# Moving the normed inputs of three groups of projections to 64 bytes above the weights' place within 512 bytes

## The reference, cut to what matters

```python
# first block, for each of 2 layers
xn = rms_norm(h, attn_norm_g[layer]);  proj = xn @ w_in[layer]          # 1024 -> 2304
...                                                                     # S5, gMLP, differential attention
h = h + mixed @ w_out[layer]
xn = rms_norm(h, ffn_norm_g[layer])
up = xn @ w_up[layer]                                                   # 1024 -> 5632
acc = causal_conv3(up);  gate, val = split(acc)
h = h + (gelu(gate) * val) @ w_down[layer]                              # 2816 -> 1024
# second block
h2 = rms_norm(x, g_pre)
a_qkv, bq, bk, bv, mq, ga, gb, gm, mg = split(h2 @ w_in_2)              # 1024 -> 10496
kvm = rms_norm(mem, g_mem) @ w_mem_kv                                   # 1024 -> 1024
ya, yb, ym = (o * silu(g)) @ w_br for the three branches
out = (sum of sigmoid(mg) * y) @ w_out_2;  x = x + rms_norm(out, g_post)
```

## The kernel before, in words

| input | read by | place | above the weights |
|---|---|---|---|
| `xth`, `xtl` | mixer's inputs, `out`, all first-level projections of the second block, `wo` | 128 | 0 |
| `fth`, `ftl` (same memory, 8 floats on) | up projections | 160 | 32 |
| `memh`, `meml` | `km`, `vm` | 128 | 0 |
| `hth`, `htl` | `down` | 128 | 0 |
| `oth`, `otl` | branches | 128 | 0 |

## Time and profile before

### The profile page before, as it was taken

One profiled execution on the slowest core, in us unless ns is written; L12 is line 12 of the kernel. 1 busy time (PEld: TensorE's weight loads), 2 busy tenths in 40 slices (PEclk: granted clock), 3 DMA queues, 4 the chain that ended last, 5 costly groups with the idle time before them and its releaser, 6 DMA issues.

```text
span 964.3 us, 15784 instructions
## 1 busy us (share of the span) xinstructions
PE 953.3 (99%) x6119; PEld 837.1 (87%) x6123; DVE 687.4 (71%) x1081; ACT 567.6 (59%) x960; POOL 232.1 (24%) x189
## 2 busy tenths in 40 slices
PE   8999999999999999999999999999999999999997
PEld 6887899999888888899999988999778889888886
DVE  7987878786765877857777754748576755666885
ACT  7967666676855657756666544535454445555733
POOL 5560203536500110302445500021131300000030
PEclk9999999999999999999999999999999999999999
DMA  8642466656664634466566565665545445754462
GB/s 299 227 131 68 142 219 186 189 178 184 194 197 152 180 127 153 133 188 192 180 194 178 195 196 154 216 202 173 166 139 153 153 144 170 199 162 155 154 180 82
DMA packets 48618, 165.96 MB, mean 172 GB/s; under 512 B 6560, under 2 KB 7072, under 8 KB 48544
## 3 DMA queue, kind: packets, MB, share of 16 engines
q1 hardware_dynamic: 48544, 164.95, 54.9%
HBM read 162.83 MB, written 1.05 MB: 170 GB/s over the span
## 4 chain that ended last, share of the span: by engine, by line
PE 88%; ACT 4%; POOL 3%; DVE 3%; issue 1%; DMA 1%; SPq 0%; DVEq 0%; POOLq 0%; ACTq 0%
PE PJ L655 14%; PE PJ L657 13%; PE PJ L656 13%; PE PJ L648 10%; PE PJ L647 10%; PE PJ L646 10%; PE PJ L593 2%; PE PJ L603 2%; PE PJ L586 2%; PE T L1118 1%; ACT sm L1378 1%; PE T L1109 1%; ACT whi L1177 1%; DMA raw<-weights_in 1%; DVE wlo L1873 1%
## 5 line engine op out<-in xcount | busy, mean ns | idle before, releaser
L1873 DVE TENSOR_TENSOR wlo<-raw,whi 128x1024 fp32r<-128x1024 f32 x294 | 368.7, 1284 | 87.2 <-ACT whi L1177 84.8
L1177 ACT ACTIVATE whi<-raw 128x1024 fp32r<-128x1024 f32 x294 | 301.6, 1059 | 64.9 <-DMA raw<-weights_in 62.5
L646 PE MATMUL PJ<-xthb,whi 128*128 128x256 f32 x832 | 233.7, 281 | 0.0
L648 PE MATMUL PJ<-xthb,wlo 128*128 128x256 f32 x832 | 233.4, 281 | 0.0
L647 PE MATMUL PJ<-xtlb,whi 128*128 128x256 f32 x832 | 232.4, 279 | 0.0
L655 PE MATMUL PJ<-whi,xthb 128*128 128x512 f32 (+1 forms) x424 | 170.8, 403 | 0.3 <-DVE wlo L1873 0.2
L657 PE MATMUL PJ<-whi,xtlb 128*128 128x512 f32 (+1 forms) x424 | 164.0, 387 | 0.0
L656 PE MATMUL PJ<-wlo,xthb 128*128 128x512 f32 (+1 forms) x424 | 164.0, 387 | 0.0
L647 PEld LDWEIGHTS PJ<-xtlb,whi 128*128 128x128 f32 x832 | 157.0, 189 | 0.3
L646 PEld LDWEIGHTS PJ<-xthb,whi 128*128 128x128 f32 x832 | 157.0, 189 | 0.3
L648 PEld LDWEIGHTS PJ<-xthb,wlo 128*128 128x128 f32 x832 | 156.9, 189 | 0.0
(11 more groups left out here) (419 smaller groups left out, 1353.2 us busy)
## 6 DMA issues: line engine op xcount, KB each, us to landing
raw<-weights_in SPq DMA_DIRECT2D x294, 512.0 KB, 3.6
rt<-bmerge_in SPq DMA_DIRECT2D x6, 256.0 KB, 4.1
memx<-mem_in SPq DMA_DIRECT2D x2, 512.0 KB, 4.0
y_out<-xn SPq DMA_DIRECT2D x4, 256.0 KB, 2.3
rowv<-rows_in SPq DMA_DIRECT2D x1, 576.0 KB, 10.5
xres<-x_in SPq DMA_DIRECT2D x2, 256.0 KB, 3.0
xres<-x_in SPq DMA_DIRECT2D x1, 512.0 KB, 7.7
ptmp<-bexp_in SPq DMA_DIRECT2D x2, 256.0 KB, 6.0
```

Source lines behind the costliest of these rows:

```text
L646: pe.matmul(o, a, xh[:, k, :], start=(first and f % 2 == 0), stop=False, skip_group_check=True)
L648: m = pe.matmul(o, b, xh[:, k, :], start=False, stop=last, skip_group_check=True)
L1177: act.activation(whi[:, p % HIGHS, :], raw[:, p % LOADS, :], ACT.Copy).then_inc(hi_ready, 1)
L1873: dve.tensor_tensor(wlo[:, p % LOADS, :], raw[:, p % LOADS, :], whi[:, p % HIGHS, :].bitcast(F32), ALU.subtract).then_inc(lo_ready, 1)
```

## The change

The instructions, their order on every engine and their waits stay as they were; only addresses change.

- `fth`, `ftl` lie 16 floats (64 bytes) into `xthb`, `xtlb`, where they lay 8.
- The second block's normed tokens (norm 5) are written to `fth`, `ftl` and read from there, where they were in `xth`, `xtl`.
- `lines` is 64 bytes longer: `memh`, `meml` go to 192, and with them every tile that is allocated behind `lines`: the first block's tables and mixer tiles, and the second block's `sm2`, `pT2`, `rt`, `gat`, `ma`, `gt` and others, all 64 bytes up.
- `lines1` and `lines2` are 64 bytes shorter, so that `hth`, `htl`, `acc`, `gtd` and `aqT`, `va`, `oth`, `otl`, `merged`, `gpost` keep their places.

Afterwards `fth`, `ftl`, `memh`, `meml` are at 192, 64 above the weights, whether they move (features first) or stand still (tokens first); `xth`, `xtl`, `hth`, `htl`, `oth`, `otl` stay at 0 above.

```diff
-                                  for o in (0, 8))
+                                  for o in (0, 16))
...
-        sbt(ctx, "lines", [P, 120])
+        sbt(ctx, "lines", [P, 136])
...
-        sbt(ffs, "lines1", [P, 96])
+        sbt(ffs, "lines1", [P, 80])
...
-        sbt(two, "lines2", [P, 96])
+        sbt(two, "lines2", [P, 80])
...
-            project("mq", fm=True, ready=(sem("xt_lo"), 80, 4))
-            project("bq")
-            project("gb", fm=True)
-            project("bkv")
+            project("mq", fm=True, xh=fth, xl=ftl, ready=(sem("xt_lo"), 80, 4))
+            project("bq", xh=fth, xl=ftl)
+            project("gb", fm=True, xh=fth, xl=ftl)
+            project("bkv", xh=fth, xl=ftl)
...
-            project("gm", fm=True)
+            project("gm", fm=True, xh=fth, xl=ftl)
...
-                    project(nm, pairs=[j], fm=nm == "ga")
+                    project(nm, pairs=[j], fm=nm == "ga", xh=fth, xl=ftl)
...
-                project(f"mg{n // 4}", pairs=[n % 4])
+                project(f"mg{n // 4}", pairs=[n % 4], xh=fth, xl=ftl)
...
-                xh = memh if n == MEM_NORM else fth if n in FFN_NORM else xth
+                xh = memh if n == MEM_NORM else fth if n in FFN_NORM or n == 5 else xth
...
-                xh, xl = (memh, meml) if n == MEM_NORM else (fth, ftl) if n in FFN_NORM else (xth, xtl)
+                xh, xl = (memh, meml) if n == MEM_NORM else (fth, ftl) if n in FFN_NORM or n == 5 else (xth, xtl)
```

## The result

The changed kernel took 969.54 us (median of 5 runs, 968.94 to 970.09), the kernel before 965.80 (5 runs, 965.09 to 966.09): ratio 1.0039, 95% interval 1.0028 to 1.0050. It is slower by 3.7 us. The forecast said 971.3 us and slower; the time lies in the range, but not for the reason given: that it came out near the forecast is luck.

A forecast was written before the change was run, and what follows sets the result against it. TensorE, busy 953.3 of 964.3 us, was taken as the bound, so start-to-start distances count one for one. Terms 5.8 - 0.4 = +5.4 us on 965.9 gave 971.3 us, range 956 to 973.

The forecast's parts named there:

- step 5: Everything else shifted 64 bytes behind `lines`, attention matmuls, transposes and other engines' tiles: 0, ends 1 us either way.
- step 4: Tokens-first matmuls leaving place 0 (768, `vm` 48, `bkv` 48 half width): stay at 226 ns, 0; end +3.4 us.
- step 1: Features-first up projections of both layers, 2016 matmuls: from 116.3 to 117.6 ns up to 120, +5.8 us.
- Step 2: First up chunk, tokens first, 48 matmuls: back from 234 to 226 ns, -0.4 us.
- Step 3: Features-first `km`, `mq`, `gb`, `gm`, `ga` leaving place 0, 480 matmuls: stay at 120 ns, 0.
- the prediction's own sign: In `a` and `mg` chunks, bursts behind attention: settling at 227 ns supports no tokens-first cost, staying at 233 refutes it.
- only place 0 is special: Every other place is like 32: up projections 117 ns, the 480 -1.3 us, tokens first +3.4; 968.0 us, chance 0.13.
- The first rival: Each further 32 bytes act like the first for the moving operand: 114.4 ns, 957.6 to 961.0 us; chance 0.37.
- The change does nothing: Tile identity or surrounding instruction order counts, not place, in all the moved products: 965.9 us, chance 0.05.
- the agreement on which I built: Tokens first, stationary operand: cost above 213 ns rises 13 to 20 ns as two 64-byte pieces become three.
- the -3 ns of the moving operand: Features first: moving input 32 bytes above the weights takes about 3 ns off each start-to-start distance.

The follow-up runs named there:

- a_sec64: Kernel before, with only the second block's normed tokens moved from 0 to 64 bytes above the weights: 967.74 us, ratio 1.0024.
- b_all_up64: Kernel before, with an unused 64-byte tile ahead of all others, so places shift but distances between operands stay: 965.72 us, ratio 1.0002.
- c_scan1: Kernel before, inputs at other distances: layer 0 up projections 16 bytes, layer 1 128, memory 128, second block 512: 965.99 against 965.69 us.
- d_scan2: Kernel before, inputs at other distances: layer 0 up projections 480 bytes, layer 1 16, memory 256, second block 496: 967.35 against 964.98 us.
- e_up448: Kernel before, with both layers' up-projection input at 448 (64 bytes below the weights) instead of 32 above: 958.6 us, ratio 0.9924.
- f_best: `e_up448` with the second block's tokens at 448 too, memory at 0: 960.23 us, ratio 0.9940 against the kernel before.
- e_all448: Kernel before, with layer 0's input and the memory at 192, layer 1's and the second block's at 448: 962.34 us, ratio 0.9963.

## Why the prediction was right or wrong

The sign was right, the mechanism was not. The forecast rested on the sentence that the operand's start counts within pieces of 64 bytes, so that 64 would be the same as 0. Every term fell but step 5, and the sum came near only because step 4 cost, at its end, much of what step 1 did not. That is luck.

- **Step 1**, +5.8 us, failed: the up projections went to 117.8 ns and not to 120, +1.0 us. (The 116.3 ns of its 288 matmuls is a count's error; by the starts they ran at 116.7.) Layer 0 left the rhythm of 116.7 for that of 117.8, which layer 1 had all along.
- **Step 2**, -0.4 us: 233 ns stayed, 0.0.
- **Step 3**, taken as 0: -1.0 us, since nothing at 64 runs at 120.
- **Step 4**, taken as 0 with an end of +3.4: the end was the truth. 768 matmuls cost 3.4 us more, `vm` 0.3 and `bkv` 0.2. The settled matmuls (471 in the prediction, 463 by the starts) and 6.5 ns each were the right sizes, but the forecast left them out. By the prediction's own sign, a burst that stays at 233 ns, this step is refuted.
- **Step 5**, 0: `a_sec64` bears it out, for what was shifted in the second block.

The rival *only place 0 is special* had 968.0 us, and its three numbers (up near 117, -1.3, +3.4) are what was measured within half a microsecond each, except that layer 0 paid 1.0 more. Its reason held in part: `b_all_up64` shows the distance, and the 512 of `c_scan1` and the 256 of `d_scan2` show what is equal to 0. But the other places are not alike: 16, 64, 192 and 448 reach 113.3 ns, which 32 did in no trace, and tokens first at 496 is no slower than at 0. The first rival, gains that grow with the distance, fell at 64 and 128. *The change does nothing* fell by the interval.

What the prediction missed stood in the earlier trace rows: 116.7 and 117.6 ns in two stretches of the same instructions at the same place. I priced each stretch by its own figure and did not ask why they differ; they said that the place alone does not fix the distance. And the agreement on which I built, 20 to 13 ns as three pieces to two, was one ratio of two numbers, with nothing to test it; the -3 ns of the moving operand did not come out of it.

## What to carry to other kernels

How far apart two operands of a matmul stream start in a partition can set its speed, with nothing else changed. Read the distance from start to start for each stretch, and where two stretches of one instruction differ, ask what differs before averaging. Here equal places let 512 moving columns settle (227 ns, against 229 to 233 in most other places) and held 256 moving columns at their slowest (120 ns, against 113 to 119 nearly everywhere else). So count the matmuls of each use before moving a tile that is moved in some products and stationary in others. A place that suits both may exist, but off the equal ones it has to be tried: 64 cost 3.4 us in the second block's tokens first and gave back 0.8 in its features first, while 496 cost nothing there and gave 1.0, less 0.3 in `bkv`, in its one run.

## What the runs showed of the hardware that was not expected

128x256 float32r matmuls at full clock kept to a few fixed distances: 113.3, 116.7, 117.8 and 120.0 ns at the places 0, 32, 64, 192 and 448. 113.3 and 117.8 were held without change through 1056 matmuls (119.70 us for those of layer 1 in `e_up448`, 124.37 after the change). At 0 only 120.0 was seen, at 32 only 116.7 and 117.8.

The choice can fall differently in two executions of the same instructions: layer 0 in `e_up448` and `f_best`, 2.3 us. `e_all448` was timed at 962.28 to 962.35 four times and at 965.79 once; that a rhythm makes this difference is likely but not shown, since only the last was profiled. A difference between two kernels of this kind below 0.5% may be a rhythm caught by chance. That is no rival for the second block's loss: its tokens-first matmuls take 183.4 to 183.5 us in both traces with place 64, and 180.0 to 180.1 in all four whose second block is at place 0 itself.

The version that beats both kernels, the up projections' input 64 bytes below the weights, gains 7.3 us against the kernel before by holding 113.3 ns in nearly all of both layers. `f_best`, the same up to the second block, shows that this is not certain in each execution.
